# Cross sums for a norm's statistic, one interleaved pass over the blocks, and modulation products in two PSUM banks, in a two-layer trunk kernel

## The chip, the cores and the metric

One Trainium2 chip, one core. The metric is the device time of the kernel in microseconds, the median of several runs.

## The reference

Two layers act on 512 tokens of width 1,024: 256 of context (`hc`) and 256 latent ones (`h`). Cut to what matters:

```python
for l in range(DEPTH):
    # m[0..8]: shift, scale and gate of three sub-layers, (silu(c) @ w_mod + b_mod)
    h = half_ffn(h, m[0], m[1], m[2], g[0], g[1], ffn1_w1, ffn1_w3, ffn1_w2)
    u = modulate(h, g[2], m[3], m[4])
    y = token_mixing(u, ...)
    h = h + m[5] * rms_norm(y, g[3])
    h = half_ffn(h, m[6], m[7], m[8], g[4], g[5], ffn2_w1, ffn2_w3, ffn2_w2)
```

`half_ffn` is `x + 0.5 * gate * rms_norm(y)` with `y = (silu(u @ w1) * (u @ w3)) @ w2`, and `modulate` is a root-mean-square norm of x times its gain and (1 + scale), plus the shift. So between two sub-layers stand two norms over the width: that of the output y (the post-norm, whose result is added to x) and that of the new x (the pre-norm of the next sub-layer). This stretch is called a gap; gap (l, j) follows sub-layer j of layer l. In the last layer the context half is not needed from the second gap on.

## The kernel before

**Layout.** The width lies on partitions in 8 blocks (KC) of 128, the 512 tokens on the free axis. x is kept in `xT`, y and then u in `uT`. Each product of fp32 numbers is three matmuls (`split_product`, L806 to L808): weights and activations are split into a rounded high part and the rest (`wh`, `wl`, `uh`, `ul`; `uTh`, `ul_in`, `wh_in`, `wl_in` for the mixer's input). Weights come in pieces of up to 1 MB into a ring of four slots, issued by SyncE in the order of a list (`PIECES`); a slot is issued again when its piece has been split, or, for a piece of `w_mod`, when its product is done. ScalarE rounds a piece (`round_piece`, L1409), VectorE subtracts (`split_rest`, L1876); the first piece after a gap is subtracted by GpSimd (`split_first`, L2505).

**Feed-forward.** Two parts, each of 11 up pieces of 48 matmuls (w1 and w3) and 8 down pieces of 33 matmuls. After the up pieces 1 to 9 of the first part and 1 to 3 of the second, in the first feed-forward, one piece of the modulation is computed (`mod_product`, L729: 16 matmuls into bank 6). ScalarE copies the row out (L1383), TensorE turns it into columns (`mod_turn`, L711), ScalarE stores them (L1388), and the next product waits for that store, because it goes to the same bank. The remaining `w_mod` pieces are spread over the gaps (three each) and the mixer, by `MOD_PLAN`. After up piece 4 of the very first part SyncE issues all the small parameters (`params`, L615 to L637): two of the constants and 30 small ones.

**Gap.** In the last part VectorE adds each down piece to y, squares it and sums the squares (`y_block`, L1955, L1958); ScalarE multiplies block by block with gate and gain (`gain`, L1424). Post-norm: two token sums on TensorE (L758, matmuls with ones), the root on ScalarE (L1414), the reciprocal on VectorE (L1916), its spread over the partitions by TensorE (`spread`, L750), and then for each block a product with the spread bank (L1969) and an addition to `xT` (L1973; blocks 2 and 5 on GpSimd, L2513, after `POOL_ADDS`). Pre-norm: ScalarE squares each new x (L1449), TensorE sums over 8 blocks, root, reciprocal, spread again, and then for each block `xT` times the bank (L1938), scale and shift (context half on ScalarE, L1468; latent half on VectorE, L1940), the rounding (L1474), the rest (L1946 on VectorE for even blocks, L2519 on GpSimd for odd ones). The first piece of the next sub-layer takes the blocks as they come. ScalarE's `round_next` rounds that first piece: for a gap after the first feed-forward it can only start with the last down matmul.

The engines run their instructions strictly in program order; only semaphores couple them.

## Time and profile before

| | |
|---|---|
| runs | 2375.47, 2375.81, 2376.28 us (median 2375.81) |
| profiled execution | 2373.44 us, span 2371.6 us, mean granted TensorE clock 0.950 |
| TensorE busy | 2174.0 us, 92% of the span |
| VectorE busy | 1095.4 us, 46% |
| ScalarE busy | 841.7 us, 35% |
| GpSimd busy | 218.1 us, 9% |

The busy shares are over the whole span. What counts for an edit is the stretch in which it lies: there, the engine that everything else waits for. L12 is line 12 of the kernel; PE is TensorE, PEld its weight load, DVE VectorE, ACT ScalarE, POOL GpSimd and SPq the queue of DMA issues of SyncE. Times of the timeline are from the span's start.

### The profile page before, as it was taken

How to read it: one execution, taken by the hardware profiler on the slowest of the kernel's cores; microseconds unless marked ns; L12 is line 12 of the kernel's file. 1: busy time of each engine (PE TensorE's matmuls, PEld its weight loads, DVE VectorE, ACT ScalarE, POOL GpSimd, SP SyncE). 2: the span in 40 equal slices, each digit the busy share in tenths (PEclk: the TensorE clock that was granted, in tenths of full speed). 3: DMA queues.
4: the chain of work that ended last, by engine and by line, in shares of the span. 5: the costliest groups of instructions: out<-in, count | busy, mean ns of one | idle time of the engine just before them, and what ended most of it. 6: DMA issues, size and time to landing. Idle time of an engine off the chain costs nothing.

```text
span 2371.6 us, 31003 instructions
## 1 busy us (share of the span) xinstructions
PE 2174.0 (92%) x13005; PEld 1800.4 (76%) x13005; DVE 1095.4 (46%) x1586; ACT 841.7 (35%) x1336; POOL 218.1 (9%) x260
## 2 busy tenths in 40 slices
PE   6889999899988898899999899999989987878997
PEld 4667878687846786688888688888868856777997
DVE  4222333576284355533333633333474475366555
ACT  3222222354345423422222432222244436334343
POOL 0000000100021342100000100000020022421000
PEclk8999999899999998999999899999978999888999
DMA  8454442422223423423432432432342312334662
GB/s 273 122 163 115 117 127 79 140 83 94 69 75 125 147 89 122 123 78 92 118 85 85 131 103 65 125 94 75 108 124 68 100 43 65 107 96 113 173 178 81
DMA packets 403323, 259.04 MB, mean 109 GB/s; under 512 B 21850, under 2 KB 401904, under 8 KB 403184
## 3 DMA queue, kind: packets, MB, share of 16 engines
q1 hardware_dynamic: 403184, 257.06, 37.3%
q8 instruction: 103, 1.69, 0.3%
q14 instruction: 36, 0.29, 0.0%
HBM read 255.97 MB, written 1.05 MB: 108 GB/s over the span
## 4 chain that ended last, share of the span: by engine, by line
PE 80%; DVE 11%; ACT 5%; issue 2%; SPq 1%; DMA 1%; POOL 1%; POOLq 0%; DVEq 0%; ACTq 0%
PE bank L806 22%; PE bank L808 21%; PE bank L807 21%; PE bank L729 2%; PE bank L1183 1%; ACT arena L1656 1%; PE bank L711 1%; PE bank L1165 1%; PE bank L1199 1%; DVE wl L1876 1%; DVE uT L1940 1%; ACT wh L1409 1%; PE bank L758 1%; DVE uT L1938 1%; PE bank L1054 1%
## 5 line engine op out<-in xcount | busy, mean ns | idle before, releaser
L806 PE MATMUL bank<-uh,wh 128*128 128x512 f32 (+1 forms) x1536 | 563.8, 367 | 34.2 <-DVE ul L1946 15.0
L807 PE MATMUL bank<-ul,wh 128*128 128x512 f32 (+1 forms) x1536 | 559.3, 364 | 0.0
L808 PE MATMUL bank<-uh,wl 128*128 128x512 f32 (+1 forms) x1536 | 559.1, 364 | 0.0
L1876 DVE TENSOR_TENSOR wl<-ring,wh 128x2048 fp32r<-128x2048 f32 (+1 forms) x157 | 317.1, 2020 | 187.7 <-ACT wh L1409 186.8
L1409 ACT ACTIVATE wh<-ring 128x2048 fp32r<-128x2048 f32 (+1 forms) x160 | 271.0, 1693 | 320.7 <-PE bank L808 305.3
L806 PEld LDWEIGHTS bank<-uh,wh 128*128 128x128 f32 x1536 | 294.9, 192 | 88.7 <-issue 34.3
L808 PEld LDWEIGHTS bank<-uh,wl 128*128 128x128 f32 x1536 | 294.3, 192 | 45.0
L807 PEld LDWEIGHTS bank<-ul,wh 128*128 128x128 f32 x1536 | 295.0, 192 | 43.7
L806 PE MATMUL bank<-hh,wh 128*128 128x512 f32 (+1 forms) x704 | 255.5, 363 | 1.4 <-DVE wl L1876 1.4
L807 PE MATMUL bank<-hl,wh 128*128 128x512 f32 (+1 forms) x704 | 255.2, 363 | 0.0
L808 PE MATMUL bank<-hh,wl 128*128 128x512 f32 (+1 forms) x704 | 255.2, 362 | 0.0
L1991 DVE TENSOR_TENSOR arena<-arena,bank 128x512 f32<-128x512 f32 (+1 forms) x88 | 54.6, 620 | 380.5 <-PE bank L808 380.5
L1508 ACT ACTIVATE hh<-arena 128x512 fp32r<-128x512 f32 (+1 forms) x88 | 50.9, 578 | 413.6 <-DVE arena L1991 413.6
L806 PEld LDWEIGHTS bank<-hh,wh 128*128 128x128 f32 x704 | 132.9, 189 | 22.4 <-DVE wl L1876 1.7
L807 PEld LDWEIGHTS bank<-hl,wh 128*128 128x128 f32 x704 | 132.9, 189 | 20.6
L808 PEld LDWEIGHTS bank<-hh,wl 128*128 128x128 f32 x704 | 132.9, 189 | 20.5
L806 PE MATMUL bank<-uTh,wh_in 128*128 128x512 f32 (+2 forms) x320 | 127.7, 399 | 11.1 <-DVE ul_in L1946 5.3
L808 PE MATMUL bank<-uTh,wl_in 128*128 128x512 f32 (+2 forms) x320 | 123.3, 385 | 0.0
L807 PE MATMUL bank<-ul_in,wh_in 128*128 128x512 f32 (+2 forms) x320 | 123.3, 385 | 0.0
L1506 ACT ACTIVATE arena<-bank 128x512 f32<-128x512 f32 (+1 forms) x88 | 47.9, 544 | 169.0 <-PE bank L808 168.9
L729 PE MATMUL bank<-ring,scT 128*32 128x256 f32 x1088 | 79.5, 415 | 26.5 <-ACT modT L1388 21.7
L1564 ACT ACTIVATE arena<-bank 128x512 f32<-128x512 f32 (+5 forms) x64 | 30.6, 480 | 176.9 <-PE bank L808 176.7
(301 smaller groups left out, 2868.6 us busy)
## 6 DMA issues: line engine op xcount, KB each, us to landing
ring<-in_ffn_w_dram SPq DMA_DIRECT2D x176, 512.0 KB, 5.2
ring<-in_w_mod_dram SPq DMA_DIRECT2D x136, 512.0 KB, 4.6
ring<-in_ffn_w_dram SPq DMA_DIRECT2D x64, 384.0 KB, 3.5
ring<-in_ffn_w_dram SPq DMA_DIRECT2D x64, 320.0 KB, 4.1
ring<-in_w_in_dram SPq DMA_DIRECT2D x40, 512.0 KB, 4.7
ring<-in_w_out_dram SPq DMA_DIRECT2D x16, 512.0 KB, 4.5
arena<-in_w_mod_dram SPq DMA_DIRECT2D x8, 512.0 KB, 9.3
ring<-in_w_in_dram SPq DMA_DIRECT2D x4, 544.0 KB, 4.6
```

Of the source, the lines that this page charges most:

```text
L711: turned = pe.matmul(bank[:, 256 + 2 * b:258 + 2 * b], mod_row[:, b * P:(b + 1) * P], cst[:, C_SEL:C_SEL + 2], start=True, stop=True)
L729: product = pe.matmul(bank[at, 256:512], scT[:, 2 * k:2 * k + 32], weights[:, k * 256:(k + 1) * 256], start=k < 4, stop=k >= 4)
L758: done = pe.matmul(bank[32 * i:32 * i + 32, 0:P], ones[:, 0:32], squares[:, i * P:(i + 1) * P], start=first, stop=last)
L806: pe.matmul(bank, w_hi, x_hi, start=first, stop=False)
L807: pe.matmul(bank, w_hi, x_lo, start=False, stop=False)
L808: return pe.matmul(bank, w_lo, x_hi, start=False, stop=last)
L1409: A(high[:, SPLIT[n] % 2, 0:floats], ring[:, n % RING, 0:floats], ACT.Copy).then_inc(wh_ready, 1)
L1506: A(silu_t[:, j % 2, t0:T], ps[2 * (j % 2)][:, t0:T], ACT.Silu).then_inc(silu_done, 1)
L1508: A(hh[:, j, t0:T], silu_t[:, j % 2, t0:T], ACT.Copy).then_inc(hh_ready, 1)
L1564: A(dst, src, ACT.Copy, scale=scale).then_inc(proj_copied, 1)
L1876: TT(low[:, b, 0:floats], at, high[:, b, 0:floats].bitcast(F32), ALU.subtract).then_inc(wl_ready, 1)
L1991: TT(ht, ht, ps[2 * (j % 2) + 1][:, t0:T], ALU.mult).then_inc(gated, 1)
```

## The change

Four things change.

1. Three of the five gaps between sub-layers are *joined*: (0,0), (0,2) and (1,0). With the new x being x + r y (y already with its gain, r the token's reciprocal root), the sum of squares of the new x is that of x, plus 2 r times the sum of x y, plus r squared times the sum of y squared. The two new sums are gathered while the last down pieces run: x y on VectorE (`cross`), y squared on ScalarE (`square_gained`) with its additions on GpSimd (`gain_sums`). In the gap the last block and three token sums follow, then five short operations on VectorE that update the statistic. The squares of x and their sums over 8 blocks go. Then one pass over the blocks interleaves update, scaling and split. Scale and shift of both halves are on ScalarE, and ScalarE rounds the second weight piece within the pass, after block 5.
2. In joined gaps two modulation pieces are computed, not three; the three others go to the second part of the first feed-forward. The second one is turned after the first piece of the next sub-layer.
3. Modulation in the feed-forward alternates between banks 6 and 7: the product of piece j is issued before the turn of piece j-1 and waits only for the store of piece j-2.
4. The small parameters are issued in six portions, after up pieces 2 to 7. In every post-norm GpSimd adds the blocks 2, 4 and 6. Some semaphores are merged.

```diff
-    MOD_PLAN = {("start", 0): RING, ("spare", 0): 4, ("ffn0", 0): 9, ("ffn1", 0): 3, ("gap0", 0): 3, ("mix", 0): 27, ("gap1", 0): 3,
-                ("gap2", 0): 3, ("gap0", 1): 3, ("mix", 1): 13}
+    MOD_PLAN = {("start", 0): RING, ("spare", 0): 4, ("ffn0", 0): 9, ("ffn1", 0): 6, ("gap0", 0): 2, ("mix", 0): 27, ("gap1", 0): 3,
+                ("gap2", 0): 2, ("gap0", 1): 2, ("mix", 1): 13}
...
-        POOL_ADDS = (2, 5)
+        POOL_ADDS = (2, 4, 6)
...
+        JOINED = [(l, j) for l in range(LAYERS) for j in (0, 2) if after(l, j)[0] < LAYERS]
+
+        def into(l, j):
+            return [a for a in JOINED if after(*a) == (l, j)]
...
+        def late_turn(l, j):
+            return gap_mods(*into(l, j)[0])[1] if into(l, j) else (None, None)
...
-                        if (l, f, part, j) == (0, 0, 0, 4):
-                            params()
+                        if (l, f, part) == (0, 0, 0) and 2 <= j < 8:
+                            params(j - 2)
...
                     rows_of.append((gpar[:, l, 32:36], ssm_d[l].partition_broadcast(P)))
-                    for dst, src in rows_of:
+                    assert PARAM_DMAS == 2 + LAYERS * len(rows_of)
+                    for dst, src in rows_of[8 * half:8 * half + 8]:
...
+            def joined(l, j):
+                first, second = gap_mods(l, j)
+                hs, q, n, i = post_halves(l, j), 3 * l + j, 6 * l + 2 * j + 1, JOINED.index((l, j))
+                if first[0] is not None:
+                    mod_product(*first, first[0])
+                pe.wait_ge(y_summed, (KC - 2) * (q + 1))
+                token_sums(ps[POST_BANK], yacc, hs, True, False)
+                pe.wait_ge(sem("xg_ready"), 2 * i + 1)
+                token_sums(ps[CROSS_BANK], xg_sum, hs, True, False)
+                pe.wait_ge(sem("gg_added"), (KC - 2) * (i + 1))
+                token_sums(ps[PRE_BANK], gg_sum, hs, True, False)
+                pe.wait_ge(y_sq, KC * (q + 1))
+                token_sums(ps[POST_BANK], ysq_of(j), hs, False, True).then_inc(sums_ready, 1)
+                pe.wait_ge(sem("gg_squared"), KC * (i + 1))
+                token_sums(ps[PRE_BANK], gg_term[:, 1, :], hs, False, True)
+                pe.wait_ge(sem("xg_ready"), 2 * i + 2)
+                token_sums(ps[CROSS_BANK], xg_last, hs, False, True).then_inc(sums_ready, 1)
+                if second[0] is not None:
+                    mod_product(*second, first[0])
+                spread(n, ps[POST_BANK], hs)
+                if first[0] is not None:
+                    mod_turn(*first)
+                spread(n + 1, ps[PRE_BANK], hs, next_inverse)
+
...
+                        if fresh and late_turn(l, 2 * f)[0] is not None:
+                            mod_turn(*late_turn(l, 2 * f))
                         if (l, f, part, j) == (0, 0, 0, SETUP_AFTER):
                             pe.wait_ge(params_in, 16 * PARAM_DMAS)
                             setup_params(1, ps[POST_BANK])
+                        g = ffn_mod(l, f, part, j)
+                        if g is not None:
+                            pe.wait_ge(y_copied, y0 + KC * part + Y_CREDIT)
+                            mod_product(g, ps[FFN_MOD_BANKS[j % 2]], g - 1 if j > 1 else g)
                         if j and ffn_mod(l, f, part, j - 1) is not None:
-                            mod_turn(ffn_mod(l, f, part, j - 1), ps[6])
-                        if ffn_mod(l, f, part, j) is not None:
-                            mod_product(ffn_mod(l, f, part, j), ps[6], ffn_mod(l, f, part, j))
+                            mod_turn(ffn_mod(l, f, part, j - 1), ps[FFN_MOD_BANKS[(j - 1) % 2]])
 
                     for j, n in enumerate(PIECES[f"down{part}", l, f]):
                         b = SPLIT[n] % 2
...
+            def square_gained(l, j, m):
+                i, q = JOINED.index((l, j)), 3 * l + j
+                act.wait_ge(y_gained, KC * q + m + 1)
+                if m >= 3:
+                    act.wait_ge(sem("gg_added"), (KC - 2) * i + m - 2)
+                dst = gg_term[:, m % 2, :] if m else gg_sum
+                A(dst, uT[:, m, :], ACT.Square).then_inc(sem("gg_squared"), 1)
+
+            def square_last(l, j, hs):
+                i, m = JOINED.index((l, j)), KC - 1
+                act.wait_ge(y_copied, y_before(l, j) + PARTS * KC + Y_CREDIT)
+                act.wait_ge(sem("gg_added"), (KC - 2) * i + m - 2)
+                for h in hs:
+                    at = slice(h * HALF, (h + 1) * HALF)
+                    last = A(gg_term[:, m % 2, at], uT[:, m, at], ACT.Square, scale=gpost[:, j, m, h:h + 1])
+                last.then_inc(sem("gg_squared"), 1)
 
...
+                    if into(l, j):
+                        A(u[:, m, CTX:T], u[:, m, CTX:T], ACT.Identity, scale=gpre[:, j, m, 1:2],
+                          bias=modT[:, l, 3 * j * KC + m, 1:2]).then_inc(u_dve, 1)
 
                     act.wait_ge(u_dve, 8 * p + m + 1)
                     if 0 in hs:
                         act.wait_ge(u_act, 8 * p + m + 1)
                     A(high[:, m, t0:T], u[:, m, t0:T], ACT.Copy).then_inc(uh_ready, 1)
+                    if m == KC - 3 and into(l, j):
+                        round_second(l, j)
                     if m == 1 and third[0] is not None:
                         mod_column_out(*third)
 
+            def round_second(l, j):
+                if j == 1:
+                    round_piece(PIECES["in", l][1], KC * IN_WIDTH[1], wh_in)
+                else:
+                    round_piece(PIECES["up0", l, j // 2][1], 2048)
+
+            def joined(l, j):
+                first, second = gap_mods(l, j)
+                hs, q, n, i = post_halves(l, j), 3 * l + j, 6 * l + 2 * j + 1, JOINED.index((l, j))
+                square_last(l, j, hs)
+                norm(n, ps[POST_BANK], hs)
+                if j == 0:
+                    round_next(l, j)
+                act.wait_ge(sem("xg_ready"), 2 * i + 2)
+                gain(l, j, KC - 1, hs)
+                if first[0] is not None:
+                    mod_row_out(*first)
+                act.wait_ge(x_squared, KC * (q + 2))
+                A(next_root, xx_sum, ACT.Sqrt, bias=epsc[:, 0:1], scale=1.0 / D).then_inc(rms_ready, 1)
+                if first[0] is not None:
+                    mod_column_out(*first)
+                    mod_row_out(*second)
+                prenorm_blocks(*after(l, j))
...
+                if n in (0, 4):
+                    V.tensor_copy(xx_sum, ps[PRE_BANK][:, 0:P])
...
+            def cross(l, j, m):
+                q, i = 3 * l + j, JOINED.index((l, j))
+                dve.wait_ge(y_gained, KC * q + m + 1)
+                first = link(TT(xg_term if m else xg_sum, xT[:, m, :], uT[:, m, :], ALU.mult))
+                if m:
+                    total = TT(xg_sum, xg_sum, xg_term, ALU.add)
+                    if m < KC - 2:
+                        link(total)
+                    else:
+                        total.then_inc(sem("xg_ready"), 1)
+
+            def cross_last(l, j, hs):
+                m = KC - 1
+                for h in hs:
+                    at = slice(h * HALF, (h + 1) * HALF)
+                    last = STT(xg_last[:, at], uT[:, m, at], gpost[:, j, m, h:h + 1], xT[:, m, at], ALU.mult, ALU.mult)
+                last.then_inc(sem("xg_ready"), 1)
+
+            def joined(l, j, hs):
+                q, n = 3 * l + j, 6 * l + 2 * j + 1
+                l2, j2 = after(l, j)
+                u, high, low = (u_in, uTh, ul_in) if j2 == 1 else (uT, uh, ul)
+                cross_last(l, j, hs)
+                norm(n, hs)
+                dve.wait_ge(inverse_ready, n + 1)
+                dve.wait_ge(sums_ready, n + 2)
+                xg, gg = ps[CROSS_BANK][:, 0:P], ps[PRE_BANK][:, 0:P]
+                link(TT(xx_term, inverse, gg, ALU.mult))
+                link(STT(xx_term, xg, 2.0, xx_term, ALU.mult, ALU.add))
+                link(TT(xx_term, xx_term, inverse, ALU.mult))
+                link(TT(xx_sum, xx_sum, xx_term, ALU.add))
+                TS(xx_sum, xx_sum, 0.0, None, ALU.max).then_inc(x_squared, KC)
+                def scaled(m):
+                    dve.wait_ge(y_gained, KC * q + m + 1)
+                    TT(uT[:, m, :], uT[:, m, :], ps[POST_BANK][:, :], ALU.mult).then_inc(y_scaled, 1)
+
+                def added(m):
+                    if m not in POOL_ADDS:
+                        dve.wait_ge(y_scaled, KC * q + m + 1)
+                        TT(xT[:, m, :], xT[:, m, :], uT[:, m, :], ALU.add).then_inc(x_ready, 1)
+
+                dve.wait_ge(inverse_spread, n + 1)
+                scaled(0)
+                dve.wait_ge(rms_ready, n + 2)
+                V.reciprocal(next_inverse, next_root).then_inc(inverse_ready, 1)
+                added(0)
+                scaled(1)
+                dve.wait_ge(inverse_spread, n + 2)
+                for m in range(KC):
+                    wait_x(dve, q, m)
+                    TT(u[:, m, :], xT[:, m, :], ps[PRE_BANK][:, :], ALU.mult).then_inc(x_scaled, 1)
+                    if m + 1 < KC:
+                        added(m + 1)
+                    if m + 2 < KC:
+                        scaled(m + 2)
+                    if m == 0 or m in (3, 5, 7):
+                        b = max(m - 1, 0)
+                        dve.wait_ge(uh_ready, split_before(l2, j2) + b + 1)
+                        TT(low[:, b, :], u[:, b, :], high[:, b, :].bitcast(F32), ALU.subtract).then_inc(ul_ready, 1)
+
...
+            def joined(l, j):
+                q, (l2, j2) = 3 * l + j, after(l, j)
+                u, high, low = (u_in, uTh, ul_in) if j2 == 1 else (uT, uh, ul)
+                for m in range(KC):
+                    if m in POOL_ADDS:
+                        pool.wait_ge(y_scaled, KC * q + m + 1)
+                        G.tensor_tensor(xT[:, m, :], xT[:, m, :], uT[:, m, :], ALU.add).then_inc(x_added, 1)
+                    if m % 2 == 0 and m:
+                        low_block(l2, j2, m - 1, u, high, low)
+                low_block(l2, j2, KC - 1, u, high, low)
+
+            def low_block(l, j, m, u, high, low):
+                pool.wait_ge(uh_ready, split_before(l, j) + m + 1)
+                G.tensor_tensor(low[:, m, :], u[:, m, :], high[:, m, :].bitcast(F32), ALU.subtract).then_inc(ul_pool, 1)
...
+            def gain_sums(l, j):
+                i = JOINED.index((l, j))
+                for m in range(1, KC - 1):
+                    pool.wait_ge(sem("gg_squared"), KC * i + m + 1)
+                    if m > 1:
+                        pool.wait_ge(sem("gg_added"), (KC - 2) * i + m - 1)
+                    G.tensor_tensor(gg_sum, gg_sum, gg_term[:, m % 2, :], ALU.add).then_inc(sem("gg_added"), 1)
...
                 if l:
+                    gain_sums(l - 1, 2)
                     split_first(PIECES["up0", l, 0][0], 2048)
                 if l:
-                    postnorm(l - 1, 2, post_halves(l - 1, 2))
-                prenorm(l, 0)
+                    joined(l - 1, 2)
+                else:
+                    prenorm(l, 0)
+                gain_sums(l, 0)
                 split_first(PIECES["in", l][0], KC * IN_WIDTH[0], (wh_in, wl_in))
-                postnorm(l, 0, post_halves(l, 0))
-                prenorm(l, 1)
+                joined(l, 0)
```

## Rows read from the trace of the kernel before

**Rows 1.** Page, part 4: the chain that ended last, its shares by engine

```profile
PE 80%; DVE 11%; ACT 5%; issue 2%; SPq 1%; DMA 1%; POOL 1%; POOLq 0%; DVEq 0%; ACTq 0%
```

**Rows 2.** The same chain in order of time, one matmul (start us, us, what)

```profile
62.35 0.23 PE bank L807
```

**Rows 3.** Timeline of SyncE: start us, us, engine, line, operation

```profile
88.84 1.63 SPq L616 DMA_DIRECT2D cst<-consts_dram  x1
...
102.47 0.35 SPq L637 DMA_DIRECT2D gpar<-in_ssm_d_dram  x1
102.87 6.51 SPq L548 DMA_DIRECT2D ring<-in_ffn_w_dram  x2
```

**Rows 4.** Timeline of TensorE and ScalarE, feed-forward; in brackets idle before and releaser

```profile
100.56 1.07 PE L729 MATMUL bank<-ring,scT 128*32 128x256 f32 x16 [1.25 <-ACT modT L1388]
...
117.16 1.91 ACT L1409 ACTIVATE wh<-ring 128x2048 fp32r<-128x2048 f32 x1 [15.09 <-DMA ring<-in_ffn_w_dram]
...
122.86 1.93 PE L729 MATMUL bank<-ring,scT 128*32 128x256 f32 x16 [9.77 <-ACT modT L1388]
...
137.16 0.51 PE L711 MATMUL bank<-cst,mod_row 128*128 128x2 f32 x4
...
150.95 0.51 PE L711 MATMUL bank<-cst,mod_row 128*128 128x2 f32 x4
```

**Rows 5.** Timeline of TensorE: last and restarting matmuls at three gaps

```profile
453.36 0.39 PE L808 MATMUL bank<-hh,wl 128*128 128x512 f32 x1
...
491.13 0.50 PE L806 MATMUL bank<-uTh,wh_in 128*128 128x512 f32 x1 [1.14 <-DVE wl_in L1876]
...
1334.16 0.39 PE L808 MATMUL bank<-hh,wl 128*128 128x512 f32 x1
...
1369.57 0.50 PE L806 MATMUL bank<-uh,wh 128*128 128x512 f32 x1 [1.08 <-DVE wl L1876]
...
1717.64 0.39 PE L808 MATMUL bank<-hh,wl 128*128 128x512 f32 x1
...
1754.02 0.79 PE L806 MATMUL bank<-uTh,wh_in 128*128 128x512 f32 x1 [1.18 <-DVE wl_in L1876]
```

**Rows 6.** Timeline of the first gap: VectorE, ScalarE and GpSimd

```profile
455.77 4.51 POOL L2505 TENSOR_TENSOR wl_in<-ring,wh_in 128x2048 fp32r<-128x2048 f32 x1 [396.73 <-ACT wh_in L1409]
455.86 0.36 ACT L1414 ACTIVATE arena<-bank,epsc 128x128 f32<-128x128 f32 x1
...
459.66 1.17 DVE L1973 TENSOR_TENSOR xT<-xT,uT 128x512 f32<-128x512 f32 x1
...
461.95 1.27 DVE L1969 TENSOR_TENSOR uT<-uT,bank 128x512 f32<-128x512 f32 x2
...
475.18 0.59 ACT L1468 ACTIVATE arena<-arena,modT,gpre 128x256 f32<-128x256 f32 x1
475.86 0.63 ACT L1474 ACTIVATE uTh<-arena 128x512 fp32r<-128x512 f32 x1
...
476.56 1.28 POOL L2519 TENSOR_TENSOR ul_in<-arena,uTh 128x512 fp32r<-128x512 f32 x1 [10.40 <-ACT uTh L1474]
476.63 1.36 DVE L1940 TENSOR_SCALAR arena<-arena,gpre,modT 128x256 f32<-128x256 f32 x1
```

**Rows 7.** Timeline of the other two gaps: one GpSimd split, two spreads

```profile
1329.17 4.59 POOL L2505 TENSOR_TENSOR wl<-ring,wh 128x2048 fp32r<-128x2048 f32 x1 [345.90 <-ACT wh L1409]
...
1337.96 1.16 PE L750 MATMUL bank<-arena,cst 128*128 128x128 f32 x8 [0.94 <-DVE arena L1916]
...
1721.55 1.88 PE L750 MATMUL bank<-arena,cst 128*128 128x128 f32 x8 [0.64 <-DVE arena L1916]
```

**Rows 8.** Groups by line and shape on VectorE: busy us, mean ns

```profile
L1916 DVE RECIPROCAL arena<-arena 128x128 f32<-128x128 f32 x9 | 8.6, 953 | 21.3 <-ACT arena L1414 21.3
...
L2237 DVE TENSOR_TENSOR uT<-bank,arena 128x128 f32<-128x128 f32 x24 | 7.0, 291 | 0.8
```

**Rows 9.** Busy time in a stretch: PE, PEld, DVE, ACT, POOL, clock, DMA

```profile
1712.00:1756.00 44.00, 33.82 (x236) 25.21 (x235) 30.07 (x49) 24.18 (x41) 13.04 (x9) 0.69 0.35 102
```

More of the change, by code:

```diff
@@ L239, in trunk @@
         yacc = view(28672, T)
+        xx_sum, xx_term, next_root, next_inverse = [view(29824 + i * P, P) for i in range(4)]
+        xg_sum, gg_sum, xg_term, xg_last = view(4096, T), view(4608, T), view(5120, T), view(7168, T)
+        gg_term = view(6144, 2, T)
         convT = view(0, 12, T)
@@ L481, in gap_mods @@
             if place not in MOD_PLAN:
-                return [(None, None)] * len(GAP_BANKS)
-            return [(MOD_FIRST[place] + i, ps[b]) for i, b in enumerate(GAP_BANKS)]
+                return [(None, None)] * (2 if (l, j) in JOINED else len(GAP_BANKS))
+            return [(MOD_FIRST[place] + i, ps[b]) for i, b in enumerate(GAP_BANKS[:MOD_PLAN[place]])]
         def quadrants(hs):
@@ L612, in _, with params @@
                     sp.dma_start(dst[:, h:h + 4, :], src[:, h:h + 4, :]).then_inc(sem(f"spare_landed{i}"), 16)
-            def params():
-                dmas = 2
-                sp.dma_start(cst[:, C_TRI:C_LEV], consts[:, C_TRI:C_LEV]).then_inc(params_in, 16)
-                sp.dma_start(cst[:, C_LEV:C_DIR], consts[:, C_LEV:C_DIR]).then_inc(params_in, 16)
-                for l in range(LAYERS):
+            def params(i):
+                if i == 4:
+                    sp.dma_start(cst[:, C_TRI:C_LEV], consts[:, C_TRI:C_LEV]).then_inc(params_in, 16)
+                if i == 5:
+                    sp.dma_start(cst[:, C_LEV:C_DIR], consts[:, C_LEV:C_DIR]).then_inc(params_in, 16)
+                if i < 4:
+                    l, half = divmod(i, 2)
                     b = prow[:, l, 1, :]
@@ L743, in mod_work, with spread @@
                         mod_turn(g, bank(g))
-            def spread(n, bank, hs):
+            def spread(n, bank, hs, source=inverse):
                 pe.wait_ge(inverse_ready, n + 1)
@@ L751, in spread @@
                                      cst[at, C_TILE + i:C_TILE + i + 1].to_broadcast([P - at.start, P]),
-                                     inverse[at, :], start=True, stop=True)
+                                     source[at, :], start=True, stop=True)
                 last.then_inc(inverse_spread, 1)
@@ L795, in postnorm @@
                 spread(6 * l + 2 * j + 1, ps[POST_BANK], hs)
+            def joined(l, j):
[21 more added lines that the diff above has]
+                spread(n + 1, ps[PRE_BANK], hs, next_inverse)
             def gap(l, j):
+                if (l, j) in JOINED:
+                    joined(l, j)
+                    return
                 first, second, third = gap_mods(l, j)
@@ L877, in proj @@
                             unit_done(last, n)
+                if late_turn(l, 1)[0] is not None:
+                    mod_turn(*late_turn(l, 1))
                 for n in range(2, NU):
@@ L1498, in ffn @@
                     for j in range(HB):
-                        if j < HB - 1:
+                        if part == 0 and j == 0 and into(l, 2 * f):
+                            pass
+                        elif j < HB - 1:
                             round_piece(up[j + 1], 2048)
@@ L1921, in prenorm @@
             def prenorm(l, j):
+                if into(l, j):
+                    return
                 hs = pre_halves(l, j)
@@ L1997, in ffn @@
                         post_gains(l, 2 * f)
+                        if (l, 2 * f) in JOINED:
+                            pre_gains(*after(l, 2 * f))
                     for j in range(KC):
@@ L2003, in ffn @@
                             split_rest(PIECES[f"up{part + 1}", l, f][0], 2048)
+                        if part == PARTS - 1 and j and (l, 2 * f) in JOINED:
+                            cross(l, 2 * f, j - 1)
                         dve.wait_ge(pieces_done, SPLIT[down[j]] + 1)
```

68 lines of the change are left out of this document (41 added, 27 removed).

## The prediction

> **What bounds the kernel now.** I read the page first. The chain that ended last is TensorE for 80% [rows 1], so the time is the matmuls, one each 0.23 us at the full clock [rows 2], plus the places where they stop. A change to any other engine counts only where TensorE waits for it. I then looked for these stops where the diff works: the timelines of SyncE and TensorE in the first feed-forward, and those of all engines in the gaps. The reader is to see three kinds of stop.
>
> First, one long stop. From 88.84 to 102.8 SyncE does nothing but issue small parameters, 32 DMAs (first and last in [rows 3]); the weight piece behind them is issued at 102.87, and ScalarE sits idle 15.09 us until it has landed, at 117.16 [rows 4]. TensorE waits 9.77 us, until 122.86, and starts again at the low clock: the 16 small matmuls take 1.93 us where they took 1.07 [rows 4].
>
> Second, a short stop in each modulation piece: the product waits 1.25 us for ScalarE's store of the piece before [rows 4].
>
> Third, the gaps. From the end of the last down matmul (its start plus 0.39) to the first matmul of the second piece it is 37.4 us, 35.0 us and 36.0 us [rows 5]. The first piece's 48 matmuls lie in this; back to back they would be 10.9 us (48 x 0.227), or half of that in the third gap, whose first units have 256 columns. So 24 to 31 us of each gap is chain between VectorE and ScalarE.
>
> **Parameters.** The 32 issues go in six portions after pieces 2 to 7. The largest holds 8 of them, at 0.35 to 1.63 us each, and lies in a time when SyncE waits for a free slot anyway; the piece behind it is rounded a whole piece (over 10 us) later. So I cost the issues at nothing; without that cover it would be the old stop. Removed: the piece that began at 101.6 (100.56 plus 1.07) should have handed on 13.79 us later (the period is 150.95 less 137.16 [rows 4]), at 115.4, but TensorE was back at 124.8. That is 9.4 us. The product and the first 8 matmuls or so at the low clock, 0.2 us each too long, are about 1.4 us more. **-10.8.** Bounds: 0 (the landing is what is slow, and it stays) and -11.5.
>
> **Modulation in two banks.** A period of 13.79 us holds 10.9 of matmuls, so a modulation piece costs 2.9; turn (0.51) and product (1.07) [rows 4] are 1.6 of it. With the next product ahead of the turn nothing waits: 1.3 to 1.4 saved, for 8 periods -10.8. In the second part it was 1.07 + 2 x 2.9 + 0.5 = 7.4 for three pieces, and will be 1.07 + 5 x 1.55 + 0.5 = 9.3 for six: +1.9. Together **-8.9**, bounds -7 (some issue time remains) and -11. The `w_mod` transfers of the three moved pieces go into a part whose rhythm is that of the first part, where the trace shows nine of them carried; cost nothing. The late turn after each joined gap stands between full matmuls: 3 x 0.5 = **+1.5**.
>
> **Gathering the sums.** In a down piece TensorE is busy for 33 x 0.227 = 7.5 us. VectorE has there a split of 1,408 columns, and three operations on 512 columns at 0.64 us (two in 1.27 [rows 6]), now five: 1.8 + 5 x 0.64 = 5.0 us. It stays under 7.5; GpSimd's addition, 1.28 us [rows 6], may hold it up once and it still fits (6.3). ScalarE gets 0.6 us more. I cost these at nothing; without the cover each us over 7.5 costs 21 us over the 21 pieces.
>
> **The front of a joined gap.** I count from s, the start of the post-norm's root, 2.1 us after the last down matmul before (455.86 against 453.75 [rows 5, 6]) and some 0.4 later now, since three token sums stand ahead. Root 0.36 [rows 6], reciprocal 0.95 [rows 8], then five short operations. The nearest row is 0.29 for 128x128 [rows 8]; with the step from one to the next 0.32, 1.6 in all. So the statistic would be there at s+3.0. Root, second reciprocal (behind the first scaling) and spread follow; the spread takes 1.16 or 1.88 [rows 7]. The pass would begin at s+6.5 to s+7.3, about 9.3 after the last matmul.
>
> Two GpSimd operations stand against that. While GpSimd subtracts a first piece (455.77, 4.51 us), an addition on VectorE with both inputs in SBUF lasts from 459.66 to 460.83, where one alone takes 0.68; it ends 0.55 after GpSimd's end. A tensor-scalar operation started at 476.63 lasts 1.36 and ends with GpSimd's of 476.56 to 477.84. The products with a PSUM bank don't wait [rows 6]. So these kinds exclude each other. In the gaps (0,0) and (1,0) ScalarE rounds the first piece directly behind the root, and GpSimd's split can start at s + 0.25 + 1.91 + 0.08 = s+2.24. The fourth short operation, SBUF with SBUF, would start at s+2.4. GpSimd is there first, by 0.1 to 0.2 us, and holds it until s+6.9. Then the statistic is there at s+7.5 and the pass begins at about 13.3, 4 us late. In gap (0,2) GpSimd's last gain sum comes ahead of its split, so that the split, 4.59 us from 1329.17 [rows 7], moves to about 1331.9 and ends 1.9 us after the last matmul; VectorE's last square (0.75) waits for it, +1.2 and some rest. The pass begins at 9.6.
>
> The Trainium skill states this as a rule ("SBUF — State Buffer", Who interferes with whom): a VectorE instruction with two SBUF inputs, or in a two-port mode, and a GpSimd instruction that reads SBUF block each other for the whole instruction, whichever issues first. The trace agrees, by the 1.17 and 1.36 us above. By the rule the gaps give 5.4 us, and without it 18 or so.
>
> **The pass.** ScalarE needs for a block two halves and the rounding: 0.42 + 0.68 + 0.53 = 1.63 us (0.59 and 0.63, with a start-to-start of 0.68 [rows 6]), plus 1.8 for the second piece: 14.9. VectorE has 8 products, 4 additions, 6 scalings and 4 splits at 0.60 to 0.64: 14. I wrote the three queues out with these steps, each addition and split excluded against GpSimd's seven operations of 1.28: the last block's rest is ready 20.9 after the pass begins, and TensorE ends the first piece at 22.4. Without exclusion it is 20.4. The second piece is then split, so its 1.1 us wait [rows 5] goes.
>
> Sum: gap (0,0) 13.3 + 22.4 = 35.7 against 37.4, -1.7. Gap (0,2) 9.6 + 22.4 = 32.0 against 35.0, -3.0. Gap (1,0), whose last matmuls are half as wide, 13.3 + 22.0 = 35.3 against 36.0, -0.7. Together **-5.4**. Bounds: 0, and -20 (9.3 + 20.4 = 29.7 in all three, less 0.4 in the last). I take the value by the exclusion, as rows show it.
>
> **Rest.** VectorE's copy of the statistic at the start and in gap (0,1): 2 x 0.25 = **+0.5**. Three blocks on GpSimd where there were two: the last addition on VectorE comes at the same time, nothing. SyncE: with two `w_mod` pieces per gap the second weight piece has its slot before the gap, which the early rounding needs.
>
> **Total.** -10.8 - 8.9 + 1.5 - 5.4 + 0.5 = -23.1. The profiled execution took 2373.44 (span 2371.6): 2350.3. The median of the runs, 2375.81, is 2.4 above it; by it 2352.7. I give 2351.
>
> **Rivals.**
> - *The short operations slip through* ahead of GpSimd's split (0.1 to 0.2 us decide): the two gaps start 4 us earlier, -7.5, or nothing is excluded in the pass either, up to -20 for the gaps. 2337 to 2345. For it: the margin is tiny. Against: the order of starts above.
> - *The joined gaps give nothing*: the pass is bound by the longer handover between three engines, or the second root comes later still. -23.1 + 5.4 = -17.7: 2357.
> - *The parameters' stop stays*, since the many tiny packets drain slowly (1 MB behind them lands 14 us after its issue). Then -12.3: 2363. Against: one portion holds a quarter, with a piece's time to land.
> - *Slower*: the clock. The span around the third gap has a granted clock of 0.69 [rows 9], between its levels 1.2 and 2.4 GHz. If the sparse work of the joined gaps leaves TensorE at 1.2 GHz, each full matmul costs 0.2 us more. To eat 23 us and 5 more it takes 140 matmuls, all 48 of the first piece in each gap and no return: from there it is slower, 2381. Before, it came back after 8 or so.
>
> **How the numbers follow.** No change and a change under 0.2% (4.8 us) can't be told apart here. Forecast 0.45; slip through 0.30; gaps give nothing 0.13; parameters stay 0.07; slower 0.02, within 0.2% 0.03 (two of the rivals at once). Faster is thus 0.95; I keep a little for what I haven't seen: 0.93, 0.04, 0.03. The forecast's own range is 2346 to 2355. The 8 in 10 range takes in the first rival and the second: 2335 to 2359.
>
> **What would show it.** Right: no ScalarE wait near 117 us; product directly ahead of turn with no wait; a period of 12.4 us; VectorE's fourth short operation lasting some 4 us in the first and third joined gap, and ending with GpSimd's split. The distance from last down matmul to second piece near 36, 32 and 35. Wrong: that distance at 30 (first rival) or above 37; first matmuls at the low clock throughout.

## The result, and the profile after

The changed kernel takes 2351.55 us (median of four runs, 2347.66 to 2354.13) against 2375.64 for the kernel before (four runs; the table ahead has three of them): a ratio of 0.9899, 95% interval 0.9882 to 0.9916, 1.0% faster. The difference of the medians is 24.1 us here. Measured a second time, with seven runs of the kernel before, it was 19.4 us (`changed_again`, below). The profiled execution has a span of 2351.1 us, 20.5 less than before.

The page of the changed kernel, its first part:

```profile
PE 2161.1 (92%) x12909; PEld 1792.0 (76%) x12909; DVE 1144.0 (49%) x1618; ACT 854.2 (36%) x1363; POOL 257.3 (11%) x284
```

TensorE is busy 13 us less: the token sums take 20.2 us where they took 29.8, the modulation products 75.1 where they took 79.5. VectorE, ScalarE and GpSimd are busy longer. None of that tells where 20 us went. The timeline of the first feed-forward does, SyncE first (columns as in [rows 3]):

```profile
75.33 0.66 SPq L654 DMA_DIRECT2D arena<-in_gdn_gnorm_dram  x2
...
77.99 0.47 SPq L654 DMA_DIRECT2D gpar<-in_ssm_d_dram  x1
78.50 5.74 SPq L562 DMA_DIRECT2D ring<-in_ffn_w_dram  x2
```

and TensorE, which answers to [rows 4]:

```profile
97.95 1.07 PE L744 MATMUL bank<-ring,scT 128*32 128x256 f32 x16
98.95 0.61 PE L726 MATMUL bank<-cst,mod_row 128*128 128x2 f32 x4
...
110.52 1.07 PE L744 MATMUL bank<-ring,scT 128*32 128x256 f32 x16
...
185.95 0.51 PE L726 MATMUL bank<-cst,mod_row 128*128 128x2 f32 x4
```

The second portion holds the weight piece behind it up by 3.2 us. The last half of that piece lands 13.2 us after its issue, and behind the fourth portion it is 12.9 us. ScalarE waits for both:

```profile
92.17 1.92 ACT L1457 ACTIVATE wh<-ring 128x2048 fp32r<-128x2048 f32 x1 [4.69 <-DMA ring<-in_ffn_w_dram]
...
116.91 1.92 ACT L1457 ACTIVATE wh<-ring 128x2048 fp32r<-128x2048 f32 x1 [4.30 <-DMA ring<-in_ffn_w_dram]
```

TensorE does not wait: VectorE has subtracted these two pieces at 96.4 and 121.2 us, and TensorE begins them at 99.4 and 124.6. So some 3 us were left in hand.

Product and turn stand back to back without an idle time, the period is 12.57 us where it was 13.79, and the low clock doesn't occur. The turn after piece 10 is at 185.95; in the kernel before it was 20.2 us later:

```profile
206.16 0.51 PE L711 MATMUL bank<-cst,mod_row 128*128 128x2 f32 x4
```

The first joined gap on TensorE (it answers to [rows 5]):

```profile
435.73 0.39 PE L850 MATMUL bank<-hh,wl 128*128 128x512 f32 x1
...
452.89 0.77 PE L848 MATMUL bank<-uTh,wh_in 128*128 128x512 f32 x1 [3.96 <-DVE ul_in L2087]
...
472.37 0.51 PE L726 MATMUL bank<-cst,mod_row 128*128 128x2 f32 x4
472.73 0.48 PE L848 MATMUL bank<-uTh,wh_in 128*128 128x512 f32 x1
```

and the same gap on VectorE and GpSimd:

```profile
440.15 0.29 DVE L2058 TENSOR_TENSOR arena<-arena 128x128 f32<-128x128 f32 x1
440.36 4.50 POOL L2683 TENSOR_TENSOR wl_in<-ring,wh_in 128x2048 fp32r<-128x2048 f32 x1 [7.23 <-ACT wh_in L1457]
440.48 4.53 DVE L2059 TENSOR_TENSOR arena<-arena 128x128 f32<-128x128 f32 x1
445.11 0.23 DVE L2060 TENSOR_SCALAR arena<-arena 128x128 f32<-128x128 f32 x1
...
448.97 0.69 DVE L2079 TENSOR_TENSOR arena<-xT,bank 128x512 f32<-128x512 f32 x1 [1.03 <-PE bank L765]
...
467.41 2.28 DVE L1982 TENSOR_TENSOR wl_in<-ring,wh_in 128x2048 fp32r<-128x2048 f32 x1
468.49 2.32 POOL L2713 TENSOR_TENSOR ul_in<-arena,uTh 128x512 fp32r<-128x512 f32 x1 [3.31 <-ACT uTh L1542]
```

GpSimd's split started 0.12 us ahead of the fourth short operation, and that operation, 0.29 us of work, took 4.53 and ended 0.15 us after the split. The last two lines show a hold that I had not written out: VectorE's split of the second piece makes GpSimd's last rest last 2.32 us where it takes 1.28, and that rest is what TensorE's first piece ends on.

Since whole executions differ by some microseconds, the kernels below are also compared by stretches that the edits touch, from the profiled execution of each: the time E at which the last down matmul before gap (0,0) ends, and from the last down matmul to the first matmul of the second piece for each joined gap. Their sum leaves out the mixers and the unjoined gaps. All in us; `changed_again` and `before_params_banks_again` run the same code as `changed` and `before_params_banks` again.

```
kernel                       E       (0,0)  (0,2)  (1,0)   sum
before                       453.75  37.4   35.0   36.0    562.1
changed                      436.12  36.6   33.5   36.9    543.1
params_at4                   447.50  36.6   32.9   36.9    554.0
params_at2                   436.28  36.6   33.6   36.9    543.4
one_bank                     451.87  36.6   33.5   36.9    558.8
before_params_banks          431.31  35.7   36.8   37.4    541.1
psum_terms                   436.73  33.6   33.7   33.9    537.9
split_early                  436.54  35.6   31.9   35.8    539.9
sum_order                    435.68  36.6   33.4   36.9    542.6
all_three                    436.08  32.6   32.8   32.8    534.2
two_edits                    435.80  32.5   32.7   32.8    533.9
two_no_adds                  435.66  32.7   32.1   32.9    533.3
changed_again                435.33  36.6   33.6   36.9    542.5
before_params_banks_again    430.76  35.7   35.0   36.0    537.4
```

How exact is this? E contains the start of the first up matmul, which lies at 46.40 to 47.76 us, differently in executions of the same code. From that matmul to E it is 406.8 us before, 388.9 to 389.0 in every kernel with both feed-forward edits and the new plan, 400.1 in `params_at4`, 405.0 in `one_bank` and 383.9 in both executions with the old plan; so these differences are good to 0.1 us. The gaps are less exact. In the five kernels that leave the joined gaps alone, (0,0) and (1,0) agree within 0.1 us, but (0,2) takes 32.9 at a granted clock of 0.84 and 33.5 to 33.6 at 0.80. The old gaps, the same code in three executions, take 35.7 to 37.4, 35.0 to 36.8 and 36.0 to 37.4.

### The profile page after: what moved, and what is told of

The parts are those of the page before. It is cut to its first block, busy times and chain, and to the rows that moved or that the text cites. A ratio compares the mean times of both kernels' runs of the same rounds, so it can differ in the third digit from the quotient of the medians.

```text
span 2351.1 us, 30953 instructions
## 1 busy us (share of the span) xinstructions
PE 2161.1 (92%) x12909; PEld 1792.0 (76%) x12909; DVE 1144.0 (49%) x1618; ACT 854.2 (36%) x1363; POOL 257.3 (11%) x284
## 3 DMA queue, kind: packets, MB, share of 16 engines
q8 instruction: 102, 1.67, 0.3%
## 4 chain that ended last, share of the span: by engine, by line
PE 81%; DVE 11%; ACT 5%; issue 1%; SPq 1%; POOL 0%; DMA 0%; POOLq 0%; DVEq 0%; ACTq 0%
PE bank L848 22%; PE bank L849 22%; PE bank L850 22%; PE bank L744 2%; PE bank L726 1%; PE bank L1231 1%; ACT arena L1762 1%; PE bank L1213 1%; PE bank L1247 1%; DVE wl L1982 1%; ACT wh L1457 1%; DVE uT L2110 1%; PE bank L1292 1%; DVE small L2401 1%; PE bank L773 1%
## 5 line engine op out<-in xcount | busy, mean ns | idle before, releaser
L848 PEld LDWEIGHTS bank<-hh,wh 128*128 128x128 f32 x704 | 132.9, 189 | 22.4 <-DVE wl L1982 1.7
L849 PEld LDWEIGHTS bank<-hl,wh 128*128 128x128 f32 x704 | 132.9, 189 | 20.5
L850 PEld LDWEIGHTS bank<-hh,wl 128*128 128x128 f32 x704 | 132.9, 189 | 20.5
L848 PE MATMUL bank<-uTh,wh_in 128*128 128x512 f32 (+2 forms) x320 | 127.2, 397 | 21.3 <-DVE ul_in L2087 10.8
L2795 POOL TENSOR_TENSOR arena<-arena 128x512 f32<-128x512 f32 x18 | 29.8, 1653 | 1040.0 <-ACT arena L1465 1040.0
L848 PEld LDWEIGHTS bank<-uTh,wh_in 128*128 128x128 f32 (+1 forms) x320 | 63.7, 199 | 41.9 <-issue 11.6
```

The lines of the kernel that those rows point to most:

```text
L848: pe.matmul(bank, w_hi, x_hi, start=first, stop=False)
L849: pe.matmul(bank, w_hi, x_lo, start=False, stop=False)
L850: return pe.matmul(bank, w_lo, x_hi, start=False, stop=last)
L2795: G.tensor_tensor(gg_sum, gg_sum, gg_term[:, m % 2, :], ALU.add).then_inc(sem("gg_added"), 1)
```

## The experiments

**The parameters in one clump, after piece 4.** The changed kernel with

```diff
-                        if (l, f, part) == (0, 0, 0) and 2 <= j < 8:
-                            params(j - 2)
+                        if (l, f, part, j) == (0, 0, 0, 4):
+                            for i in range(6):
+                                params(i)
```

> The changed kernel with the 32 parameter issues in one clump after up piece 4 again. Theory A (the clump's place, in front of a weight piece that is then late, made the stop): the stop of ScalarE near 115 us comes back and the time is about 11 us over the changed kernel's 2351.5, 2362; first-part distance from the first matmul of piece 1 to the turn after piece 10 back from 123.8 to about 134.5 us. Theory B (with the shorter period the same clump would be hidden, and the gain lies elsewhere): under 3 us.

Measured: 2360.58 us (ratio to before 0.9947, 0.9929 to 0.9965), 9.0 over the changed kernel's median with six runs from 2357.44 to 2369.18, and 10.9 in the sum of stretches. The wait is back, on the timeline of ScalarE:

```profile
116.57 1.91 ACT L1458 ACTIVATE wh<-ring 128x2048 fp32r<-128x2048 f32 x1 [16.27 <-DMA ring<-in_ffn_w_dram]
```

and TensorE waits behind it:

```profile
120.86 0.79 PE L849 MATMUL bank<-uh,wh 128*128 128x512 f32 x1 [8.48 <-DVE wl L1983]
```

Theory A holds.

**The clump after piece 2.** The same edit with `== (0, 0, 0, 2)`.

> The changed kernel with the whole clump after up piece 2, where SyncE otherwise waits 12 us for a free slot. Theory A1 (issue time in front of the next weight piece is what counts): the clump, 14 us, covers that idle time almost exactly, so at most 2 us over the changed kernel. Theory A2 (the tiny packets drain slowly and hold up the piece behind, wherever they stand): a weight piece lands some 8 to 14 us late, but it has a whole piece of time in hand, so 0 to 6 us over it. Portions were needed only if this is over 3 us.

Measured: 2352.98 us, 0.3 in the sum. The 32 issues run from 47.2 to 60.0, and the weight piece behind them is issued at 62.23, when its slot is free. It lands late, so that ScalarE waits, but not TensorE:

```profile
77.19 1.92 ACT L1458 ACTIVATE wh<-ring 128x2048 fp32r<-128x2048 f32 x1 [2.06 <-DMA ring<-in_ffn_w_dram]
```

So both mechanisms exist, the issue time and the slow landing, and together they fit into one piece's slack if the clump stands in SyncE's idle time. Portions alone don't remove the slow landing: behind 32 DMAs the last half of the weight piece lands 13.8 us after its issue (kernel before), behind the seven of the second portion 13.2, behind the eight of the third 5.9. Six portions weren't needed; the place was.

**One bank.** The changed kernel with turn before product, both in bank 6:

```diff
-    FFN_MOD_BANKS = (6, 7)
+    FFN_MOD_BANKS = (6, 6)
...
-                        g = ffn_mod(l, f, part, j)
-                        if g is not None:
-                            pe.wait_ge(y_copied, y0 + KC * part + Y_CREDIT)
-                            mod_product(g, ps[FFN_MOD_BANKS[j % 2]], g - 1 if j > 1 else g)
                         if j and ffn_mod(l, f, part, j - 1) is not None:
-                            mod_turn(ffn_mod(l, f, part, j - 1), ps[FFN_MOD_BANKS[(j - 1) % 2]])
+                            mod_turn(ffn_mod(l, f, part, j - 1), ps[6])
+                        if ffn_mod(l, f, part, j) is not None:
+                            mod_product(ffn_mod(l, f, part, j), ps[6], ffn_mod(l, f, part, j))
```

> The changed kernel with turn first, then product, both in bank 6 again, in the feed-forward. Theory: 1.22 us per piece return for the 8 later pieces of the first part and the 5 of the second, 15.9 us: 2367. Rival (the wait of 1.25 us was partly hidden, or the second bank costs a wait elsewhere): under 8 us.

Measured: 2366.74 us (0.9969, 0.9959 to 0.9978), 15.2 over the changed kernel's median and 15.7 in the sum. The list of waits of TensorE from 60 to 345 us (total, times, longest) has the line that the changed kernel hasn't:

```profile
PE bank L744 <- ACT modT L1434: 14.9, 12, 1.3
```

**The two edits alone, with the old gaps.** The kernel before with the portions and the two banks; `MOD_PLAN` and the gaps untouched.

> The kernel before, with only the portions and the two banks; its gaps stay, with three modulation pieces each, and three in the second part. Theory (the joined gaps give next to nothing in sum): 10.7 + 8 x 1.22 + 2 x 1.22 = 22.9 us under the kernel before, 2353, within 3 us of the changed kernel. Rival (the joined gaps carry the 5 us forecast or more): 2357 or above.

Measured: 2350.05 us (0.9896, 0.9881 to 0.9911), not slower than the whole change. It reaches gap (0,0) 4.8 us earlier, since three modulation pieces fewer are in the second part; counted from the first up matmul it is 5.0, three times the 1.67 us of a piece.

**Short operations in PSUM.**

```diff
+                term = ps[CROSS_BANK][:, P:2 * P]
                 link(TT(xx_term, inverse, gg, ALU.mult))
-                link(STT(xx_term, xg, 2.0, xx_term, ALU.mult, ALU.add))
-                link(TT(xx_term, xx_term, inverse, ALU.mult))
-                link(TT(xx_sum, xx_sum, xx_term, ALU.add))
-                TS(xx_sum, xx_sum, 0.0, None, ALU.max).then_inc(x_squared, KC)
+                link(STT(term, xg, 2.0, xx_term, ALU.mult, ALU.add))
+                link(TT(term, term, inverse, ALU.mult))
+                link(TT(term, xx_sum, term, ALU.add))
+                TS(xx_sum, term, 0.0, None, ALU.max).then_inc(x_squared, KC)
```

> The changed kernel with the intermediate term of the five short operations in a free part of a PSUM bank, so that the fourth has one SBUF input and the fifth reads PSUM. The same operations, the same order, the same waits. Theory (VectorE and GpSimd exclude each other): the fourth operation takes 0.3 us, not 4.5, in gaps (0,0) and (1,0); the addition of block 0 then waits for GpSimd's split instead, so the pass begins about 3 us earlier in each, 6 us in sum: 2345. Rival (it waited for a semaphore or for data that come with the split's end): 4.5 us stay, 0 us.

Measured: gaps (0,0) and (1,0) 3.0 us shorter each. The median, 2349.40, fell by 2.2 us, where the theory said 6; the interval of the ratio (0.9877 to 0.9912) is 8 us wide and can't tell the two apart. VectorE and GpSimd in the first gap:

```profile
440.97 4.51 POOL L2684 TENSOR_TENSOR wl_in<-ring,wh_in 128x2048 fp32r<-128x2048 f32 x1 [7.22 <-ACT wh_in L1457]
441.10 0.29 DVE L2060 TENSOR_TENSOR bank<-arena,bank 128x128 f32<-128x128 f32 x1
441.50 0.29 DVE L2061 TENSOR_SCALAR arena<-bank 128x128 f32<-128x128 f32 x1
441.70 0.68 DVE L2064 TENSOR_TENSOR uT<-uT,bank 128x512 f32<-128x512 f32 x1
...
443.16 2.87 DVE L2069 TENSOR_TENSOR xT<-xT,uT 128x512 f32<-128x512 f32 x1
```

The same fourth operation at the same place beside the same GpSimd operation now takes 0.29 us. No semaphore has changed, only where the intermediate term lies, which is the fourth operation's second input and its result. The two operations behind it (L2061, L2064) write to SBUF beside the same GpSimd operation and aren't held, so what held the fourth was the second SBUF input and not the place of its result. The first operation behind it that has two SBUF inputs (L2069) is held instead.

**The second split earlier.** In the pass, `split_rest` of the second piece stands before the rest of block 6 (and no longer at the head of the next section):

```diff
+                    if m == KC - 1:
+                        if j2 == 1:
+                            split_in(l2, 1)
+                        else:
+                            split_rest(PIECES["up0", l2, j2 // 2][1], 2048)
                     if m == 0 or m in (3, 5, 7):
...
```

> The changed kernel with VectorE's split of the second piece before its rest of block 6, in the 2 us in which it waits for ScalarE, not after it. Theory (that split, 2.28 us, held GpSimd's last rest up by 1.04 us, which ends the first piece): the last rest lasts 1.28 us, not 2.32, and each joined gap is 1.0 us shorter, 3 us in sum. Rival (the last rest is bound by ScalarE's rounding of block 7): no change in the gaps' length.

Measured: gaps 1.0, 1.5 and 1.1 us shorter; 2346.57 us (0.9885, 0.9866 to 0.9904). In gap (0,2) the granted clock was 0.84 in place of 0.80, which goes with 0.5 of the 1.5. GpSimd's last rest:

```profile
468.92 1.29 POOL L2720 TENSOR_TENSOR ul_in<-arena,uTh 128x512 fp32r<-128x512 f32 x1 [3.30 <-ACT uTh L1542]
```

**The split ahead of the last gain sum.**

```diff
-                    gain_sums(l - 1, 2)
+                    gain_sums(l - 1, 2, range(1, KC - 2))
                     split_first(PIECES["up0", l, 0][0], 2048)
+                    gain_sums(l - 1, 2, range(KC - 2, KC - 1))
```

> The changed kernel with GpSimd's split of the first piece ahead of its last gain sum in gap (0,2). Theory: VectorE's square of the last block takes 0.69 us, not 2.14, and the gap is 1.4 us shorter; the other gaps keep their length. Rival: the last sum comes later now and TensorE waits for it instead, 0 us. Read from the trace, since the time can't tell 1.4 us.

A miss, read from one profiled execution (2354.30 us): gap (0,2) is 0.1 us shorter. In the changed kernel the split began at 1314.90 and held the last square:

```profile
1318.33 2.14 DVE L2125 TENSOR_TENSOR arena<-uT 128x512 f32<-128x512 f32 x1
```

With the edit it begins 5.4 us ahead of the end of the last down matmul, in place of 2.7, and holds an operation ahead of that square:

```profile
1313.75 4.62 POOL L2683 TENSOR_TENSOR wl<-ring,wh 128x2048 fp32r<-128x2048 f32 x1 [4.64 <-ACT wh L1457]
...
1314.50 4.42 DVE L2032 TENSOR_TENSOR arena<-xT,uT 128x512 f32<-128x512 f32 x1 [0.60 <-ACT uT L1489]
...
1321.23 0.69 DVE L2125 TENSOR_TENSOR arena<-uT 128x512 f32<-128x512 f32 x1
```

The square is short again, but late: the cross product ahead of it in VectorE's order took the hold, and the square ended 2.8 us after the last down matmul, as before (2.9).

**All three, and the two that worked.**

> The three edits together: terms in PSUM, the early split, the split ahead of the last sum. Theory: 6 + 3 + 1.4 = 10 us under the changed kernel, 2341. Rival (they fight for the same engine, GpSimd, and the gain is that of the largest): 5 to 6 us.

> The changed kernel with the terms in PSUM and the early split, without the new order of GpSimd's sums. The three joined gaps should be 32.5, 32.2 and 32.8 us long from the last down matmul to the second piece; the median about 2342, the same as with all three edits, since the new order gave nothing in the gap it was for.

Measured: 2340.16 us with all three (0.9858, 0.9836 to 0.9879), 2340.64 with two (0.9868, 0.9854 to 0.9883). Both are faster than the kernel before and than the changed kernel. The edits add up: 543.1 less 5.2 less 3.2 would be 534.7, and it is 533.9 to 534.2.

**No additions on GpSimd.** The two edits and

```diff
-        POOL_ADDS = (2, 4, 6)
+        POOL_ADDS = ()
```

> The two edits, and GpSimd adds no block: VectorE adds all eight in every post-norm. If the holding of the port costs less than the work that GpSimd takes over (3 x 0.6 us), the pass gets longer by 1 to 2 us in each joined gap. If it costs more, the pass gets shorter: three additions of GpSimd hold VectorE up by 0.6, 0.8 and 0.8 us in the trace, 2.2 us against 1.8, so I expect within 0.5 us of the same, and 0.5 us more in each unjoined gap.

Measured: 2339.85 us (0.9862, 0.9846 to 0.9879), 0.6 less in the sum. All of that is in gap (0,2), at a granted clock of 0.84 against 0.79, and can be the clock's; the other two gaps are 0.1 us longer. Three additions taken over by GpSimd buy nothing in the pass. They take three operations of 0.68 us from VectorE, and in the first gap VectorE is held 2.2 us in the pass with them and 1.4 us without (the split of the first piece left out).

**The references again, on one chip.**

> The changed kernel again, as the measure for the other three on the same chip: 2351.

> The kernel before with portions and two banks again. By the stretches that don't hold a mixer it is 2 us shorter than the changed kernel: 2349, at the edge of what five rounds tell.

Measured: 2352.91 us (0.9918, 0.9904 to 0.9933) for the changed kernel, 2347.67 (0.9899, 0.9884 to 0.9913) for the old gaps with portions and banks. The kernel before has a median of 2372.31 here, so the change is worth 19.4 us in this measurement, not 24.1. The medians differ by 5.2 us and the sums of stretches by 5.1, in favour of the old gaps; the intervals of the two ratios still overlap.

## Why the prediction was right

**Parameters, -10.8.** From the first feed-forward's start to the turn after piece 10 it is 20.5 us less; 8 periods of 1.22 are 9.8 of it, so the stop was 10.7. `params_at4` puts 10.9 back. Right in place and size. The reason holds for TensorE alone: I had the piece behind a portion rounded a whole piece, over 10 us, later, and ScalarE was waiting for it already; TensorE had 3 us in hand. So one of the signs, "no ScalarE wait near 117 us", did not come: it waits 4.30 us until 116.91. The rival that the stop stays is out, though the slow landing it spoke of is real (`params_at2`, and the second and fourth portion).

**Two banks, -8.9.** Measured -9.8 and +2.6, together -7.2. The mechanism is right (`one_bank`), a size was off: the period without wait is 12.57, so a modulation piece costs 1.67 us and not 1.55; 0.1 of handing over remains.

**The copy at the start, +0.25.** Not shown. The first up matmul of piece 1 is 0.28 later, but its time scatters by 1.4 us from execution to execution.

**The front of the joined gap.** The pass was to begin 13.3, 9.6 and 13.3 us after the last down matmul; it began at 12.8, 9.7 and 12.8. The step that the forecast turned on, that GpSimd's split would get in ahead of the fourth short operation by 0.1 to 0.2 us and hold it for 4 us, came out: 0.12 and 4.53. `psum_terms` shows the cause, as against a wait for data. In gap (0,2) the last square took 2.14 us where it takes 0.69.

**The pass, 22.4 to the end of the first piece.** Measured 23.4, and in the third gap 23.3 where I had 22.0. The step that failed: my three queues ended with the pass and left out the split of the second piece behind it, 2.28 us on VectorE, which gets in ahead of GpSimd's last rest and holds it 1.04 us. `split_early` takes just that back. So the joined gaps with their late turns gave 0.8 and 1.6 us and cost 0.9, -1.4 in all against the forecast's -3.9. That is against the one execution of the kernel before; the same old gaps took 1.4 us more and 1.7 us less in sum in the two executions of `before_params_banks`, so the size of this gain, and its sign, are not shown.

Sum: -10.7 - 7.2 - 1.4 + 0.3 = -19.0 by the stretches, against -23.1. A term that neither the forecast nor this sum has lies behind gap (1,0). From the second piece to the last matmul of the mixer's input projection it is 132.8 to 132.9 us in all three executions with the old gaps and 129.8 to 130.1 in the six with an unedited gap (1,0): 2.8 us less, at a granted clock of 0.91 against 0.89. Before, the second piece began with twelve full matmuls at the low clock, in the changed kernel with five. With it the two profiled executions are 21.8 us apart in what is counted; the first mixer and what follows it up to gap (0,2) gives 1.4 of that back, and the spans differ by 20.5.

The medians differ by 24.1 us in the first measurement and by 19.4 in the second. From the second piece after gap (0,0) to the last down matmul before gap (0,2), the first mixer mostly, the 14 profiled executions took 839.1 to 849.1 us, with no order by kernel, and that is scatter enough for both. That the first median came within 1 us of the forecast is luck of that size; by the second the gain was some 4 us smaller than forecast. Each step that the forecast has is right within 2.5 us.

**What the forecast didn't ask.** The joined gaps need the second weight piece early, so three `w_mod` pieces had to leave the gaps, where they filled waits, for the feed-forward, where they cost 5.0 us (first up matmul to E, `before_params_banks` against the changed kernel). Counted with that, joining the gaps cost 2 to 5 us in the sum of stretches; with the 2.8 us behind gap (1,0) it is between 2 us gained and 3 us lost, by the pair of executions one takes. No gain is shown. Where did it go? On the timeline of the kernel before, TensorE starts the first piece here:

```profile
476.14 0.77 PE L806 MATMUL bank<-uTh,wh_in 128*128 128x512 f32 x1 [2.67 <-DVE ul_in L1946]
```

22.4 us after the last down matmul (20.7 in the two executions of `before_params_banks`). In the joined gap it starts at 16.8 (13.6 in gap (0,2)), 3.9 to 5.6 us earlier, and even with the hold. But its first piece then lasts 19.5 us instead of 13.9: update, addition, scaling and split go through VectorE, ScalarE and GpSimd block by block, 2.4 us a block, where before only the scaling and split stood there. It is the blocks and not the clock that set these 19.5 us: in `params_at4` they are 19.5 too, with a granted clock of 0.92 in place of 0.76; TensorE is then busy for 14.2 of them in place of 16.2 and waits for the rest. The work was moved behind the restart, not away. With the two holds removed the exchange pays: `two_edits` is 3.5 us under `before_params_banks_again` in the sum, and 7.0 in the medians.

The slower rival, the clock, came in part and did not decide. In gap (0,0) the first 19 matmuls of the first piece are at the low clock, where it was 7, and in gap (0,2) 16 where it was 12. In gap (0,0) it cost nothing, since the blocks set the length: with only 6 at the low clock (`params_at4`) it is 36.6 us as well. In the old gaps the clock explains the scatter: gap (0,2) took 36.8 us in one execution of the same code and 35.0 in another, at a granted clock of 0.77 and 0.80, and gap (0,0) 37.4 and 35.7, at 0.77 and 0.81.

## What to carry to other kernels

Before giving work to GpSimd, write out which VectorE instructions beside it have two SBUF inputs; a long GpSimd operation that starts 0.1 us ahead of a short one on the critical chain can cost its whole length (4.2 us here), and moving one operand to PSUM can undo it (3.0 us of it here, since a later operation was held instead). A pass that saves a statistic but makes the consumer wait block by block has to be priced to the end of the consumer's first piece, with the instruction that follows the pass in each queue; and a stretch behind it can change by the clock (2.8 us here). Small parameter DMAs belong where the issuing queue is idle, whether in portions or not.

## What the hardware showed that I had not expected

The hold goes both ways, and in the rows above whichever started first kept the other waiting until it had ended: VectorE's fourth operation lost 4.2 us to GpSimd's split, and GpSimd's last rest 1.04 us to VectorE's. Operations reading one input from SBUF and one from PSUM, or PSUM alone, ran beside GpSimd at full speed (0.29 and 0.68 us), reciprocals too (0.94). The Trainium skill states both ("SBUF — State Buffer", Who interferes with whom): a VectorE instruction with two SBUF inputs contends with a GpSimd instruction that reads SBUF, and one with at most one SBUF input, outside the two-port modes, does not. These rows agree with it. Ahead of the prediction it says that only semaphores couple the engines; for VectorE and GpSimd this case shows that it isn't so, since the hold on the fourth operation goes away in `psum_terms`, which changes no semaphore.

An issue of a small parameter DMA takes SyncE 0.25 to 0.5 us in most rows, the same for the same parameter, and the 32 of them take 12.8 to 14.0 us.

Most of the 10 us scatter of the long stretch goes with TensorE's clock. The mixer alone, from the last matmul of its input projection to the first of the next feed-forward, took 276.0 us in `params_at4` and 283.1 in `changed_again`, the same code there. Length, busy time and instructions of TensorE, its weight loads, VectorE, ScalarE and GpSimd, then the granted clock and the DMA:

```profile
618.18:894.18 276.00, 235.97 (x2102) 185.60 (x2102) 149.01 (x342) 120.63 (x310) 75.68 (x108) 0.96 0.35 108
607.55:890.65 283.10, 243.18 (x2103) 191.25 (x2102) 149.07 (x342) 121.00 (x310) 75.65 (x108) 0.92 0.34 105
```

The same matmuls are busy 7.2 us longer, at a lower granted clock, and the other engines as long as before. Whole executions show it too: the six of `params_at4` go from 2357.44 us at a mean granted clock of 0.956 to 2369.18 at 0.947. In the other executions the mixer lies between these two lengths and these two clocks. Why one execution has more of the low clock than another isn't shown.
